# A two-block transformer kernel on one core: a new order at the start of four feed-forwards, a first weight chunk in halves, the rotary set-up moved, and the final norm of the first block computed together with the norm behind it

## The reference, cut to what matters

```python
# first block: two layers, 256 tokens, width 1024
for i in range(DEPTH):
    h = h + 0.5 * swiglu(rmsnorm(h, ffn1_norm[i]), gate, up, down)      # stage ffn1
    h = h + concat(mla, mlstm, fnet)(rmsnorm(h, mix_norm[i])) @ w_out   # stage mix1
    h = h + 0.5 * swiglu(rmsnorm(h, ffn2_norm[i]), gate, up, down)      # stage ffn2
    e = rmsnorm(p[i] @ ple_w_proj[i], ple_post_norm[i])
    h = h + sigmoid(rmsnorm(h, ple_gate_norm[i]) @ ple_w_gate[i]) * e   # stage ple
x = rmsnorm(h, final_norm)                                              # stage final
# second block: x and a context stream ctx, both 256 tokens; its first step (stage ffn_a):
x   = x   + 0.5 * mx2 * swiglu(rmsnorm(x, g) * (1 + mx1) + mx0, w1, w2)
ctx = ctx + 0.5 * mc2 * swiglu(rmsnorm(ctx, g) * (1 + mc1) + mc0, w1, w2)
```

## Time and profile before

| what | value |
|---|---|
| runs, us | 3434.3, 3443.83, 3443.45; median 3443.45 |
| profiled execution | 3430.92 us; its span 3429.1 us |
| granted clock of PE, mean | 0.98 |
| PE busy | 3297.9 us, 96% of the span |
| DVE, ACT, POOL busy | 46%, 36%, 2% |
| the 4 feed-forwards of the first block, PE's first matmul at | 17, 399, 636, 1010 us |
| ple of layer 1, end of its matmuls | 1246.7 us |
| ffn_a, first chunk | 1277.9 us |

### The profile page before, as it was taken

How to read it: one execution, slowest core, us unless ns; L and a number is a source line. 1 busy time by engine, 2 the same in 40 slices (tenths; PEclk the granted TensorE clock), 3 DMA queues, 4 the chain that set the end, 5 groups by cost and what they waited for, 6 DMA issues and landing times. The chain is left out here.

```text
span 3429.1 us, 56473 instructions
## 1 busy us (share of the span) xinstructions
PE 3297.9 (96%) x23726; PEld 2863.7 (84%) x23726; DVE 1564.9 (46%) x2285; ACT 1226.8 (36%) x1823; POOL 53.7 (2%) x67
## 2 busy tenths in 40 slices
PE   7999999999999989999999899999999999999899
PEld 7997799899779978888788788858888888876799
DVE  5544455564345543223674555523233422337444
ACT  4343334434333452222643334322222422233433
POOL 0000000100000010000000000000000000000000
PEclk9999999999999989999999999999999999999999
DMA  6446544444644522222222222212222222211353
GB/s 237 159 160 233 191 179 170 172 175 157 255 177 175 178 100 98 98 98 94 91 86 80 108 99 100 100 62 98 98 95 93 83 98 98 88 67 55 111 184 123
DMA packets 62913, 439.21 MB, mean 128 GB/s; under 512 B 6672, under 2 KB 9872, under 8 KB 10000
## 3 DMA queue, kind: packets, MB, share of 16 engines
q1 hardware_dynamic: 61552, 435.43, 34.8%
q10 hardware_dynamic: 1184, 1.18, 0.1%
HBM read 435.53 MB, written 1.05 MB: 127 GB/s over the span
## 5 line engine op out<-in xcount | busy, mean ns | idle before, releaser
L641 ACT ACTIVATE sb_w_split<-sb_ring 128x2048 fp32r<-128x2048 f32 x264 | 505.1, 1913 | 1042.8 <-PE ps_low L458 854.3
L649 DVE TENSOR_TENSOR sb_w_split<-sb_ring,sb_w_split 128x2048 fp32r<-128x2048 f32 x264 | 604.5, 2290 | 546.2 <-ACT sb_w_split L641 546.2
L458 PE MATMUL ps_low<-sb_x_split,sb_w_split 128*128 128x256 f32 (+1 forms) x4224 | 709.6, 329 | 38.5 <-DVE sb_w_split L649 27.5
L458 PEld LDWEIGHTS ps_low<-sb_x_split,sb_w_split 128*128 128x128 f32 x4224 | 633.3, 195 | 104.8 <-issue 21.7
L458 PE MATMUL ps_high<-sb_x_split,sb_w_split 128*128 128x256 f32 (+1 forms) x4224 | 690.2, 323 | 0.6 <-DVE sb_w_split L649 0.6
L458 PEld LDWEIGHTS ps_high<-sb_x_split,sb_w_split 128*128 128x128 f32 x4224 | 618.1, 190 | 62.6 <-DVE sb_w_split L649 0.8
L458 PE MATMUL ps_low<-sb_a_split,sb_w_split 128*128 128x256 f32 (+1 forms) x2112 | 372.4, 326 | 12.6 <-DVE sb_arena L1142 9.1
L458 PE MATMUL ps_high<-sb_a_split,sb_w_split 128*128 128x256 f32 (+1 forms) x2112 | 369.4, 324 | 0.0
L458 PEld LDWEIGHTS ps_low<-sb_a_split,sb_w_split 128*128 128x128 f32 x2112 | 315.2, 191 | 52.0 <-issue 14.4
L458 PEld LDWEIGHTS ps_high<-sb_a_split,sb_w_split 128*128 128x128 f32 x2112 | 315.5, 191 | 30.4
L458 PE MATMUL ps_low<-sb_xn,sb_ring 128*128 128x256 f32 (+1 forms) x800 | 185.7, 390 | 1.8 <-ACT sb_xn L2264 1.8
(11 more groups left out here) (319 smaller groups left out, 3087.5 us busy)
## 6 DMA issues: line engine op xcount, KB each, us to landing
sb_ring<-weights SPq DMA_DIRECT2D x411, 1024.0 KB, 4.8
sb_consts<-consts SPq DMA_DIRECT2D x1, 2017.0 KB, 15.3
sb_h<-xT SPq DMA_DIRECT2D x1, 1024.0 KB, 7.3
sb_h<-ctxT ACTq DMA_DIRECT2D x1, 1024.0 KB, 17.2
out<-sb_h SPq DMA_DIRECT2D x1, 1024.0 KB, 4.8
sb_vectors<-vectors SPq DMA_DIRECT2D x1, 269.0 KB, 2.7
sb_arena<-positions ACTq DMA_DIRECT2D x1, 128.0 KB, 7.0
```

The lines of the kernel that those rows point to most:

```text
L458: ins = self.g.nc.tensor.matmul(out, lhsT, rhs, start=start, stop=stop)
L641: g.nc.scalar.activation(g.w_split[:, 0, s % 2, :], g.ring[:, n % SLOTS, :], ACT.Copy).then_inc(g.sem["w_high"], 1)
L649: g.nc.vector.tensor_tensor(g.w_split[:, 1, s % 2, :], g.ring[:, n % SLOTS, :], g.w_split[:, 0, s % 2, :].bitcast(F32), ALU.subtract).then ...
```

## The change

1. ACT runs one small Square ahead of the wait for the inputs. Chunk 0 is split in two halves, k = 0 to 3 and k = 4 to 7, and PE waits for the second half only at k = 4.
2. In the four feed-forwards of the first block, split 4 is put ahead of Silu 0 to 3 on ACT and ahead of products 0 and 1 on DVE, and split 5 behind the four.
3. `setup_scalar` and `setup_vector` go behind the last split of the first feed-forward.
4. In ffn2 of layer 1 ACT squares the other stream's 8 tiles, POOL adds them.
5. In ple of layer 1 ACT makes two squares of each tile, of `h` and of `h` times the final gain, POOL adds both kinds for tiles 0 to 6, and both chunk splits of ffn_a move in. ACT also scales the other stream there, and runs a small Sqrt ahead of the last tile's squares. PE sums columns for all three kinds at once; the second norm's mean square is worked out from the gained sum and the first reciprocal. ffn_a then skips its own squares and sums, and the normed main stream is written to `h` behind ffn_a's input.

```diff
+def first_split_high(act):
+    act.wait_ge(g.landed[0], 16)
+    for half in range(2):
+        high, _, whole = first_split(g, half)
+        name = "w_high" if half else "first_high"
+        g.nc.scalar.activation(high, whole, ACT.Copy).then_inc(g.sem[name], 1)
...
@@ plain_ffn_tensor, first_gates
+            if first and k == KT // 2:
+                pe.wait_ge(g.used[0], 1)
@@ plain_ffn_scalar
     split_high(act, 2)
     split_high(act, 3)
     plain_root_scalar(act, others=2)
-    silu(0)
-    silu(1)
-    pair(1)
+    split_high(act, 4)
+    for f in range(4):
+        silu(f)
+    split_high(act, 5)
+    if kind == "ffn2" and l == LAYERS - 1:
+        other_squares_scalar(act)
     with act.engine.Fori(0, (PAIRS_FF - 3) // 2) as it:
         for p in range(2, 4):
             pair(p, it)
-    if kind == "ffn1" and l == 0:
-        setup_scalar(act)
...
     with act.engine.Fori(0, 2) as it:
         for c in range(1, 5):
             ahead(c, it)
+    if kind == "ffn1" and l == 0:
+        setup_scalar(act)
@@ plain_ffn_vector
     scaled_gate(0)
     scaled_gate(1)
+    split_low(dve, 4)
     product(0)
     product(1)
-    pair(1)
+    scaled_gate(2)
+    scaled_gate(3)
+    product(2)
+    product(3)
+    split_low(dve, 5)
...
@@ ple_vector, behind scaled(j) and finish(j - 1)
+        if j in ((5,) if last else (6, 7)):
+            dve.chunks += chunk_count(kind)
+            split_low(dve, 1 if j == 7 else 0)
+            dve.chunks -= chunk_count(kind)
     finish(KT - 1)
+    if last:
+        dve.chunks += chunk_count(kind)
+        split_low(dve, 1)
+        dve.chunks -= chunk_count(kind)
...
+def final_squares_scalar(act, ready, between):
+    act.wait_ge(g.sem["final_sum"], KT - 1)
+    for j in range(KT):
+        A(g.xn[:, j, TOK:2 * TOK], g.h[:, j, TOK:2 * TOK], ACT.Copy, scale=g.mod(0)[:, 1, j, 1:2])...
+        if j == KT - 1:
+            A(g.root[:, 10:11], g.eps[:, 0:1], ACT.Sqrt)...
+        ready(j)          # Sigmoid of tile j + 1, then the wait for h of tile j
+        A(b["plain"][:, j, :], g.h[:, j, 0:TOK], ACT.Square)...
+        A(b["gained"][:, j, :], g.h[:, j, 0:TOK], ACT.Square, scale=gain[:, j:j + 1])...
+        between(j)        # split_high of ffn_a's chunk 0 at j = 4, of chunk 1 at j = 6
...
+def final_tensor(pe, l, kind):
+    pe.wait_ge(g.sem["final_sum"], FINAL_ADDS)     # 19 additions on POOL
+    for at, name in ((2, "other"), (0, "plain"), (4, "gained")):
+        for t in range(TOK // P):
+            pe.mm(tile[:, at + t:at + t + 1], b[name + "_sum"][:, t * P:(t + 1) * P], ones, at == 2 and t == 0, False)
+    pe.wait_ge(g.sem["final_square"], 2)
+    ...               # 4 more one-column matmuls, the squares of tile 7
+def final_rows_tensor(pe):
+    pe.wait_ge(g.sem["norm_rinv"], pe.due("norm_rinv"))
+    ...               # 4 row blocks to a low bank, 2 to a high bank
+def final_scalar(act, l, kind):
+    ...               # Sqrt of 128 x 4; scaled(0), scaled(1); wait; Sqrt of 128 x 2; scaled(2) to scaled(7)
+def final_vector(dve, l, kind):
+    ...               # reciprocal, two products, wait for the second root, reciprocal, product
+def final_rows_vector(dve):
+    for k in range(KT):
+        ins = g.nc.vector.scalar_tensor_tensor(g.h[:, k, 0:TOK], g.h[:, k, 0:TOK], gain[:, k:k + 1], rows[:, 0:TOK], ALU.mult, ALU.mult)
...
@@ ffn2_vector
+    if kind == "ffn_a" and l == 0:
+        norm_low_vector(dve, i, width, "final_scaled")
+        final_rows_vector(dve)
@@ program, scalar
+            act.wait_ge(g.sem["vec_step"], 1)
+            g.nc.scalar.activation(g.root[:, 0:1], g.eps[:, 0:1], ACT.Square)...
-                                 between=lambda j: split_high(act, 0) if j == 3 else None)
+                                 between=lambda j: first_split_high(act) if j == 3 else None)
```

More of the change, by code:

```diff
@@ L987, in first_gates @@
     def first_gates():
-        w = [part.rearrange("p (k n) -> p k n", k=KT) for part in weights(0)]
+        first = kind == "ffn1" and l == 0
+        if first:
+            pe.wait_ge(g.sem["first_low"], 1)
+            w = [g.w_split[:, part, 0, :] for part in range(2)]
+        else:
+            w = weights(0)
+        w = [part.rearrange("p (k n) -> p k n", k=KT) for part in w]
         for f in range(2):
@@ new lines, in other_squares_scalar, with final_add_pool @@
+def other_squares_scalar(act):
+    g = act.g
+    for j in range(KT):
+        g.nc.scalar.activation(final_buffers(g)["other"][:, j, :], g.h[:, j, TOK:2 * TOK],
+                               ACT.Square).then_inc(g.sem["other_square"], act.adds("other_square"))
+def final_add_pool(pool, name, j):
+    g = pool.g
+    b = final_buffers(g)
+    if "final_sum" in pool.made:
+        pool.wait_ge(g.sem["final_sum"], pool.made["final_sum"])
+    other = b[name][:, 0, :] if j == 1 else b[name + "_sum"]
+    g.nc.gpsimd.tensor_tensor(b[name + "_sum"], b[name][:, j, :], other, ALU.add).then_inc(g.sem["final_sum"], pool.adds("final_sum"))
@@ new lines, in other_sum_pool, with final_sum_pool @@
+def other_sum_pool(pool):
+    for j in range(1, KT):
+        pool.wait_ge(pool.g.sem["other_square"], j + 1)
+        final_add_pool(pool, "other", j)
+def final_sum_pool(pool):
+    for j in range(KT - 1):
+        pool.wait_ge(pool.g.sem["square_in"], pool.due("square_in", 2))
+        if j:
+            final_add_pool(pool, "plain", j)
+            final_add_pool(pool, "gained", j)
+FINAL_ADDS = 3 * KT - 5
+def final_tensor(pe, l, kind):
+    g = pe.g
+    b = final_buffers(g)
+    pe.wait_ge(g.sem["high_free"], pe.tiles["high"] - 3)
+    tile = pe.open("high")
+    ones = g.const("ones")[:, 0:1]
+    pe.wait_ge(g.sem["final_sum"], FINAL_ADDS)
[3 more added lines that the diff above has]
+    pe.wait_ge(g.sem["final_square"], 2)
+    for at, name in ((0, "plain"), (4, "gained")):
+        for t in range(TOK // P):
+            end = at == 4 and t == TOK // P - 1
+            pe.mm(tile[:, at + t:at + t + 1], b[name][:, KT - 1, t * P:(t + 1) * P], ones, False, end, full="high" if end else None)
@@ new lines, in final_scalar @@
+    act.wait_ge(g.sem["final_cols"], 1)
+    act.wait_ge(g.sem["high_full"], act.tiles["high"] + 1)
+    tile = act.tile("high", peek=True)
+    act.other_frees("high")
+    A(g.root[:, 0:4], tile[:, 0:4], ACT.Sqrt, scale=1.0 / D, bias=g.eps[:, 0:1]).then_inc(g.sem["final_root"], act.adds("final_root"))
+    scaled(0)
+    scaled(1)
+    act.wait_ge(g.sem["final_mean"], 1)
+    A(g.root[:, 8:10], g.root[:, 4:6], ACT.Sqrt, scale=1.0 / D, bias=g.eps[:, 0:1]).then_inc(g.sem["final_root"], act.adds("final_root"))
@@ L3773, in _ @@
             act = Engine(g, scalar)
+            act.wait_ge(g.sem["vec_step"], 1)
+            g.nc.scalar.activation(g.root[:, 0:1], g.eps[:, 0:1], ACT.Square).then_inc(g.sem["act_step"], act.adds("act_step"))
             act.wait_ge(g.sem["vectors_in"], act.due("vectors_in", 16))
```

137 lines of the change are left out of this document (103 added, 34 removed).

## The result

The kernel after takes 3402.71 us (median of four executions, 3391.55 to 3413.1), the kernel before 3442.36 on the same chip. The ratio is 0.989 with an interval of 0.985 to 0.992. The forecast was 3400 us, with a range of 3386 to 3416. The profiled executions differ by less than forecast: 3430.92 and 3403.53, 27.4 us where the sum of the parts was 40.8.

The account below looks back on a forecast made before the run. PE bounds, waiting for chunks' low parts and DVE's L1142, with its largest hole at the last norm. 3.1 + 16.2 - 0.4 + 7.0 + 14.9 = 40.8 us off median and mean gives 3402.7 and 3397.3; named 3400, range 3386 to 3416.

Parts of the forecast that it names:

- Start: Start of the kernel: table load ahead of x's arrival and chunk 0 in halves gain 3.1 us, between 1.8 and 3.3.
- The late landing of chunk 0: At the start: if chunk 0 lands only by 12.73, not by 11.45, the start's gain loses 1.28 us.
- Gates: Four feed-forwards: stall moves from chunk 4 to chunk 5, shrinks to 0.2 us; 4.05 us each, 16.2 in all.
- the 0.4 us taken off: Last feed-forward instance: a POOL addition can hold up DVE's split 6, 0.4 us lost without cover.
- Rival B: Gates: the stall stays at chunk 5, PE idles 2.2 us, 14.8 us are given back, time 3415; chance 10%.
- C: Rival, gate loop: entered late without recovering, DVE or ACT behind per chunk; at 0.75 us each, time 3454; chance 2%.
- Set-up: First feed-forward: moving the set-up behind the last split gains 7.0 us, between 6 and 7.3.
- Last norm: From ple's last tiles to ffn_a: DVE's first product comes at 1260.3 instead of 1275.17, gaining 14.9 us.
- one sign: Last norm, in the profile after: DVE's first product some 13.5 us behind the scaling of tile 7, instead of 28.4.
- Rival A: Last norm: POOL's last addition is held behind DVE's split of chunk 1, sum 2.6 us later, time 3403.6; chance 10%.
- The step that failed: Stages the change does not touch, mix1 among them: counted as keeping their time, 0 us.

Follow-up runs that it names:

- run 6: Kernel after with one more POOL addition ahead of tile 6's additions in the last norm: 3418.05 us, one execution.
- the repetition: Kernel after measured once more with nothing edited: 3412.37 us, ratio 0.991 to the kernel before.
- the three parts alone: Kernel before with one part each: gate order 3425.94 us (0.9958), last norm 3427.48 us (0.9956), start and set-up 3430.54 us (0.9978).
- run 7: Extra matmuls of unused product at the head of each mix1: 6 in kernel before, 3449.26 us (1.0041); 2 in kernel after, 3404.33 us (0.990).
- run 5: Kernel after without the small Square at the start and the small Sqrt in the last norm: 3409.44 us, one execution.
- both shifted ones: Kernel after with 2 extra matmuls heading each mix1, 3404.33 us; the same plus earlier split 5 and earlier column sums, 3405.41 us.

## Why the prediction was right, and which step was not

**Start.** The late landing of chunk 0 was the open bound; it had landed, and 3.2 us came against 3.1.

**Gates.** As counted: the stall went from chunk 4 to chunk 5, 0.18 us of it is left (forecast 0.2), and the clock no longer falls. From each instance's first matmul to its chunk 5 it is 4.19, 3.90, 4.04 and 4.03 us less (forecast 4.05 each). In ffn2 of layer 1 two additions of POOL were held up behind splits (2.2 and 2.6 us instead of 0.73) and split 6 took 2.44 us instead of 2.29, but PE lost nothing by it, so the 0.4 us taken off were not needed. Rival B did not come, nor C: the feed-forwards behind chunk 5 keep their pace.

**Set-up.** 6.9 us against 7.0. At its new place it starts at 203.88, behind the last split, and ends at 207.8 where DVE's next work begins (207.70), so that less than 0.3 of it shows. The ones-sum of the next stage comes at 216.78, on time.

**Last norm.** The sum was right to 0.1 us, and so was each link. The stage starts 14.26 us earlier in the trace after; with that added, POOL's sums, PE's rows and DVE's first product stand at 1251.98, 1258.16 and 1260.28, where 1252.0, 1258.15 and 1260.3 were forecast. Only one sign was mis-stated: the product was to come 13.5 us behind tile 7's scaling and came 12.8 behind it. The 13.5 were counted from the scaling's place before the change, but it comes 0.7 us later now, behind split 0. The sum doesn't use that scaling. Rival A was missed by 0.56 us, where 0.6 had been counted; its price of 2.6 was too high: the hold cost 1.9 in run 6.

**The step that failed** is a term put at nothing without a reason: the sum takes for granted that all stages the change does not touch keep their time. Most do: in these two traces none but mix1 moved by more than 0.7 us, but for 1.4 us over the last 1,122. For mix1 they do not: 7.5 us longer in layer 0, 5.0 in layer 1, because its clock is lower in the profile after. So the sum of 40.8 us was reached locally (41.6, of which 0.33 by the earlier x), and 27.4 arrived. The median still agreed with the forecast, partly by luck: it stands on four executions, and the repetition gave 3412.4 in place of 3402.7, in the upper part of the range. The two measurements say 38 and 31 us, the three parts alone 37.

**What is shown and what is not.** It is shown that the long mix1 needs none of the changed code (run 7, in the kernel before) and does not follow it always (run 5, layer 0). It is shown that each long stage has its first fall at or just behind the same 32 matmuls, and that their place against the grid of the clock's changes sorts all 26 stages. The change moved these matmuls by 14.7 us in layer 0, and in the changed kernel they stood off the stretch of the grid where the stage is short in nine of ten unshifted stages; in the kernel before they stood on it in all four. In layer 1 of the changed kernel the stage is long in all five unshifted profiles and short in both shifted ones, but the grid lay elsewhere in those executions too, so how much of that is the shift's doing is not shown. In layer 0 every long stage stood in a kernel with the moved set-up; its stages too are sorted by the table, and the set-up was not tried by itself. What makes the second block's mixing stage take 652 or 667 us was not looked into beyond its clock.

## What to carry to other kernels

Put a chunk's split ahead of everything that may come later on its engine: that gives back the idle time and, on top, the slow clock behind it (here 2.5 us of wait and 1.6 us of slow clock, four times). Read the price of a local edit from its own stage and then compare every other stage between the traces, since an untouched one moved by 5 and 7.5 us here, and another by 15.7 between two executions of one kernel. Where an untouched stage has changed, look up where the clock falls in it and which matmuls stand there: the place at which the short and the long executions part is more telling than the stage's start. Before a small operation is added on POOL, look for the long DVE operation that may begin ahead of it: here 0.56 us stood between the full gain and a loss of 1.9 us.

## What the runs showed of the hardware

- The clock can fall while PE has no gap: from 227.2 to 234.0 us PE was busy 6.80 of 6.80 us at a granted clock of 0.50, and 2.77 of 2.77 us in the matmuls of 16 columns ahead of it; the same matmuls in the kernel before were followed by a clock at full level.
- In each of the 13 traces all changes of the granted clock stand on one even grid, to 0.01 us, and the grid's place against the kernel's start differs between executions. In mix1 the place of 32 matmuls of 16 columns against it separates 12 short stages (1.14 to 1.83 us behind a grid point) from 14 long ones (0.34 to 0.84, 2.20 and 2.57).
- A wait of 2.51 us before chunk 4 was followed by a chunk at a mean granted clock of 0.77 that took 7.3 us instead of 5.76; without the wait it ran at 1.00.
- The mixing stage of the second block took 651.7 and 667.3 us in two executions of one kernel, with a clock of 0.98 and 0.95.
- 5.2 us of added matmuls cost 14.1 us (9 to 19) in the kernel before; in its profile one mix1 stage had become 7 us longer.
- A table load took 1.28 us and nothing visible behind it: on the path it cost 1.3 and 1.4 us (run 5).
- An addition of 128 x 256 on POOL that begins behind the start of DVE's split of 128 x 2048 ended 0.6 us behind the split (the earlier trace rows and run 6) and took about 2 us more.
